# Quads of pool_out and down: another order of the seven products, their loads and sums, y pieces and squares at other steps, and a rewritten last normalization

## The reference, cut to what matters

```python
def pool_mixer(...):                       # ... mixed, scale, g are [256, 4096]
    return (mixed * scale * jax.nn.silu(g)) @ w_out          # y [256, 4096] @ w_out [4096, 2048]

def conv_ffn(...):                         # y [256, 5504] @ w_down [5504, 2048]
    ...

x = x + conv_ffn(rms_norm_2(x, norm_ffn[l]), w_up[l], conv_w[l], conv_b[l], w_down[l])
return rms_norm_2(x, norm_final)           # x * rsqrt(mean(x*x) + 1e-6) * g
```

## Time and profile before

| | |
|---|---|
| median of three runs | 2447.51 us (2446.94 to 2447.71) |
| profiled execution | 2447.4 us, its span 2445.6 us |
| TensorE busy | 2431.4 us, 12682 matmuls |
| VectorE busy | 1688.9 us |
| ScalarE busy | 1361.1 us |
| GpSimd busy | 64.3 us |
| granted TensorE clock | 0.999 |
| DMA | 453.03 MB, mean 185 GB/s |

### The profile page before, as it was taken

How to read it: one execution, slowest core, us unless ns; L and a number is a source line. 1 busy time by engine, 2 the same in 40 slices (tenths; PEclk the granted TensorE clock), 3 DMA queues, 4 the chain that set the end, 5 groups by cost and what they waited for, 6 DMA issues and landing times.

```text
span 2445.6 us, 34055 instructions
## 1 busy us (share of the span) xinstructions
PE 2431.4 (99%) x12682; PEld 2087.0 (85%) x12682; DVE 1688.9 (69%) x2037; ACT 1361.1 (56%) x1804; POOL 64.3 (3%) x79
## 2 busy tenths in 40 slices
PE   9999999999999999999999999999999999999998
PEld 8888888877889999888888888888988888888886
DVE  7675757899765655656656767665767667689886
ACT  6444444555656655556755556565644545456554
POOL 0000000001000000010000000000000000000010
PEclk9999999999999999999999999999999999999999
DMA  8666666565556654565585564455566666656654
GB/s 312 199 189 188 181 190 188 173 231 182 189 174 180 180 156 139 207 210 190 168 232 165 158 177 144 167 177 155 173 190 181 189 191 179 195 169 203 218 185 138
DMA packets 234627, 453.03 MB, mean 185 GB/s; under 512 B 14961, under 2 KB 60449, under 8 KB 233356
## 3 DMA queue, kind: packets, MB, share of 16 engines
q1 hardware_dynamic: 230992, 435.94, 57.3%
q0 software_dynamic: 3120, 14.90, 1.7%
q10 hardware_dynamic: 396, 0.59, 0.2%
HBM read 448.68 MB, written 2.69 MB: 185 GB/s over the span
## 4 chain that ended last, share of the span: by engine, by line
PE 95%; DVE 4%; ACT 1%; issue 0%; DMA 0%; SPq 0%; ACTq 0%; DVEq 0%
PE ps L779 24%; PE ps L781 13%; PE ps L745 12%; PE ps L747 12%; PE ps L746 12%; PE ps L929 4%; PE ps L931 4%; PE ps L930 4%; DVE w_lo L2361 1%; PE ps L703 1%; PE ps L812 1%; PE ps L811 1%; PE ps L810 1%; PE ps L1381 1%; DVE w_lo L2353 0%; PE ps L1141 0%
## 5 line engine op out<-in xcount | busy, mean ns | idle before, releaser
L2353 DVE TENSOR_TENSOR w_lo<-raw,w_hi 128x1024 fp32r<-128x1024 f32 x702 | 861.0, 1233 | 504.7 <-ACT w_hi L1551 484.0
L1551 ACT ACTIVATE w_hi<-raw 128x1024 fp32r<-128x1024 f32 x702 | 740.6, 1060 | 676.9 <-PE ps L781 357.2
L779 PE MATMUL ps<-x_hi_lo,w_hi 128*128 128x512 f32 x2336 | 820.9, 394 | 0.5 <-DVE w_lo L2353 0.5
L781 PE MATMUL ps<-x_hi_lo,w_lo 128*128 128x256 f32 x2336 | 660.7, 283 | 0.0
L779 PEld LDWEIGHTS ps<-x_hi_lo,w_hi 128*128 128x128 f32 x2336 | 438.7, 188 | 102.0 <-DVE w_lo L2353 0.8
L745 PE MATMUL ps<-w_hi,x_hi_lo 128*128 128x512 f32 (+3 forms) x1248 | 487.2, 390 | 0.0
L747 PE MATMUL ps<-w_hi,x_hi_lo 128*128 128x512 f32 (+3 forms) x1248 | 478.9, 384 | 0.0
L746 PE MATMUL ps<-w_lo,x_hi_lo 128*128 128x512 f32 (+3 forms) x1248 | 477.9, 383 | 0.0
L781 PEld LDWEIGHTS ps<-x_hi_lo,w_lo 128*128 128x128 f32 x2336 | 439.2, 188 | 0.0
L1728 ACT ACTIVATE w_hi<-raw 128x1024 fp32r<-128x1024 f32 (+1 forms) x184 | 189.2, 1041 | 164.4 <-PE ps L931 130.7
L747 PEld LDWEIGHTS ps<-w_hi,x_hi_lo 128*128 128x128 f32 x1248 | 234.5, 188 | 42.2
(11 more groups left out here) (442 smaller groups left out, 2563.3 us busy)
## 6 DMA issues: line engine op xcount, KB each, us to landing
raw<-in_w_up SPq DMA_DIRECT2D x160, 512.0 KB, 4.0
raw<-in_pool_w_in SPq DMA_DIRECT2D x126, 512.0 KB, 4.0
raw<-in_w_in SPq DMA_DIRECT2D x96, 480.0 KB, 3.7
raw<-in_w_down SPq DMA_DIRECT2D x82, 512.0 KB, 5.0
raw<-in_pool_w_out SPq DMA_DIRECT2D x64, 512.0 KB, 4.6
raw<-in_ple_w_gate SPq DMA_DIRECT2D x64, 512.0 KB, 4.2
raw<-in_mla_w_in SPq DMA_DIRECT2D x56, 448.0 KB, 3.5
raw<-in_pool_w_group SPq DMA_DIRECT2D x32, 512.0 KB, 4.1
```

The source lines that it names most:

```text
L779: pe.matmul(bank, w_hi[:, slot, cols], xs[:, k].rearrange("p s n -> p (s n)"), start=k == 0, stop=False, skip_group_check=True)
L781: last = pe.matmul(bank[:, 0:T], w_lo[:, slot, cols], xs[:, k, 0, :], start=False, stop=k == nkt - 1, skip_group_check=True)
L1551: act.activation(w_hi[:, t.slot(), :], raw[:, slot, :], ACT.Copy).then_inc(S("w_hi"), 1)
L2353: dve.tensor_tensor(w_lo[:, t.slot(), :], raw[:, u % RAW, :], w_hi[:, t.slot(), :].bitcast(F32), ALU.subtract)\
```

## The change

The quads' products go in the order b11, T2, b22, T3, T1, b21, T4 on all engines. The sums are formed as T2 = b22 - b12, T3 = T2 + b11, T1 = b22 - T3, T4 = b21 - T3. The four loads come as b12, b22, b11, b21, with another table of releases. The first quad of pool_out comes one plain step later in pair 0. TensorE waits for all banks of both sets at the first quad or the first plain step of the pair's second chunk, whichever comes first. The squares of columns 1 and 0 go behind later steps (pool_out: from 6, 7 to 15, 17; down: from 8, 9 to 23, 26), the y pieces of down behind steps 6, 7, 11, 13, 17, 22 instead of 6 to 11, and the first PSUM reads of pool_out's pair 0 one step later. In the ending the first three columns' sums and the 1e-6 are put together ahead for both halves, the root takes the last column's sum with scale 1/D and that as bias, and VectorE adds the second half's last columns between the two pieces it scales for the first half.

```diff
-POOL_OUT = [P0[:9] + PQ[0] + P1[:3] + PQ[1] + P1[3:6] + PQ[2] + P1[6:] + P0[9:],
+POOL_OUT = [P0[:9] + P1[:1] + PQ[0] + P1[1:4] + PQ[1] + P1[4:7] + PQ[2] + P1[7:] + P0[9:],
+DOWN_Y_STEPS = {6: 3, 7: 4, 11: 5, 13: 6, 17: 7, 22: 8}
@@ quad_tables
-                loads += [(j1, 2 * p), (j1, 2 * p + 1), (j2, 2 * p + 1), (j2, 2 * p)]
-                released += [products + 3, products + 3, products + 5, products + 6]
+                loads += [(j1, 2 * p + 1), (j2, 2 * p + 1), (j1, 2 * p), (j2, 2 * p)]
+                released += [products + 1, products + 4, products + 6, products + 6]
@@ tensor: quad
                     block(e1, "e1", x.yh[:, y1, t0], x.yl[:, y1, t0], last)
+                    block(e7, "e7", x.sums_hi[0][:, q], x.sums_lo[:, 0, q], last)
                     block(x.bank(c + 1, 0), (c + 1, 0), x.sums_hi[2][:, q], x.sums_lo[:, 2, q])
+                    block(e6, "e6", x.sums_hi[1][:, q], x.sums_lo[:, 1, q], last)
                     block(e5, "e5", x.yh[:, y1, t1], x.yl[:, y1, t1], last)
-                    block(e7, "e7", x.sums_hi[0][:, q], x.sums_lo[:, 0, q], last)
                     block(x.bank(c, 0), (c, 0), x.yh[:, y2, t0], x.yl[:, y2, t0])
-                    block(e6, "e6", x.sums_hi[1][:, q], x.sums_lo[:, 1, q], last)
                     block(x.bank(c, 1), (c, 1), x.yh[:, y2, t1], x.yl[:, y2, t1])
@@ tensor: the steps of a pair
                 for kind, c, kts in steps:
+                    if (kind == "quad" or c == 2 * p + 1) and begins("all sets"):
+                        for s in range(2):
+                            pe.wait_ge(S(f"mm_free{s}"), t.at(f"set{s}", 1))
...
-                        if c == 0:
-                            for s in range(2):
-                                pe.wait_ge(S(f"mm_free{s}"), t.at(f"set{s}", 1))
-                            if p == 0:
-                                pe.wait_ge(S(split), x.tiles.index("sums") + 1)
+                        if c == 0 and p == 0:
+                            pe.wait_ge(S(split), x.tiles.index("sums") + 1)
@@ scalar: step_hi
-                product_hi(loaded(0))
                 product_hi(loaded(2))
                 product_hi(summed(0, 1))
-                product_hi(summed(1, 2))
+                product_hi(loaded(1))
+                product_hi(summed(2, 2))
+                product_hi(summed(1, 3))
                 product_hi(loaded(3))
-                product_hi(summed(2, 3))
                 product_hi(summed(3, 4))
@@ scalar: squares and y pieces
-            if n == 6:
+            if n == 15:
                 square_mixed(1)
-            if n == 7:
+            if n == 17:
                 square_mixed(0)
...
-            if 6 <= n < 3 + len(DOWN_Y):
-                y_hi(n - 3)
+            if n in DOWN_Y_STEPS:
+                y_hi(DOWN_Y_STEPS[n])
...
-            if n in (8, 9):
-                square_out(9 - n)
+            if n in (23, 26):
+                square_out((26 - n) // 3)
@@ scalar: the ending
-            act.sem_inc(S("last_sums"), 1)
-            act.wait_ge(S("last_mean_square"), tt + 1)
-            act.activation(rt[:, 12, tt:tt + 1], ms[:, 12, tt:tt + 1], ACT.Sqrt).then_inc(S("last_root"), 1)
+            act.wait_ge(S("last_mean_square"), 1)
+            act.activation(rt[:, 12, tt:tt + 1], sums[:, 12, tt, 3:4], ACT.Sqrt, scale=1.0 / D, bias=ms[:, 12, tt:tt + 1])\
+               .then_inc(S("last_root"), 1)
@@ vector: step_lo
-            b11, b12, b22, b21 = (raw[:, (u + n) % RAW, :] for n in range(4))
-            product_lo(b11)
-            dve.wait_ge(S(f"raw_full{(u + 1) % RAW}"), 16 * ((u + 1) // RAW + 1))
-            dve.tensor_tensor(b11, b12, b11, ALU.subtract).then_inc(S("w_sums"), 1)
-            product_lo(b22)
+            b12, b22, b11, b21 = (raw[:, (u + n) % RAW, :] for n in range(4))
+            sums_before = t.n.get("w_sums", 0)
+            for n in range(2):
+                dve.wait_ge(S(f"raw_full{(u + n) % RAW}"), 16 * ((u + n) // RAW + 1))
             dve.tensor_tensor(b12, b22, b12, ALU.subtract).then_inc(S("w_sums"), 1)
             product_lo(b11)
+            dve.wait_ge(S("w_sums"), sums_before + 1)
+            dve.tensor_tensor(b11, b12, b11, ALU.add).then_inc(S("w_sums"), 1)
+            product_lo(b12)
+            product_lo(b22)
+            dve.wait_ge(S("w_sums"), sums_before + 2)
             dve.tensor_tensor(b22, b22, b11, ALU.subtract).then_inc(S("w_sums"), 1)
-            product_lo(b12)
+            product_lo(b11)
+            product_lo(b22)
             product_lo(b21)
-            dve.wait_ge(S("w_sums"), t.n.get("w_sums", 0) + 3)
-            dve.tensor_tensor(b21, b21, b22, ALU.subtract).then_inc(S("w_sums"), 1)
-            product_lo(b22)
+            dve.tensor_tensor(b21, b21, b11, ALU.subtract).then_inc(S("w_sums"), 1)
             product_lo(b21)
@@ vector: the ending
-        for tt in range(2):
+        link(dve.reduce_sum(ms[:, 12, :], sums[:, 12, :, 0:3], AXX))
+        dve.tensor_scalar(ms[:, 12, :], ms[:, 12, :], 1.0 / D, EPS, ALU.mult, ALU.add).then_inc(S("last_mean_square"), 1)
+        def last_columns(tt):
...
+        last_columns(0)
+        for tt in range(2):
             dve.wait_ge(S("last_root"), tt + 1)
             dve.reciprocal(rstd[:, 12, tt:tt + 1], rt[:, 12, tt:tt + 1]).then_inc(S("last_rstd"), 1)
             dve.wait_ge(S("last_rstd"), tt + 1)
+            dst = h[:, tt, 1024:1536]
+            dve.tensor_scalar(dst, dst, rstd[:, 12, tt:tt + 1], None, ALU.mult).then_inc(S("final_added_out"), 1)
+            if tt == 0:
+                last_columns(1)
+            dst = h[:, tt, cols]
+            dve.scalar_tensor_tensor(dst, dst, rstd[:, 12, tt:tt + 1], fgain[:, cols], ALU.mult, ALU.mult).then_inc(S("final_added_out"), 1)
```

More of the change, by code:

```diff
@@ L2830, in _ @@
                 y_lo(n - 4)
-            if n in (20, 21):
-                quads_mixed(0, n - 20)
+            if n in (21, 22):
+                quads_mixed(0, n - 21)
         for n in (2, 3):
@@ L3378, in _ @@
                 dve.wait_ge(S("y_pairs"), 15)
-            if 6 <= n < 3 + len(DOWN_Y):
-                y_lo(n - 3)
+            if n in DOWN_Y_STEPS:
+                y_lo(DOWN_Y_STEPS[n])
             if 28 <= n <= 28 + 3:
@@ L3402, in _ @@
             dve.tensor_tensor(h[:, tt, cols], h[:, tt, cols], down.bank(NCH - 1, tt), ALU.add).then_inc(S("last_added"), 1)
-            dve.wait_ge(S("last_sums"), tt + 1)
-            link(dve.reduce_sum(ms[:, 12, tt:tt + 1], sums[:, 12, tt:tt + 1, :], AXX))
-            dve.tensor_scalar(ms[:, 12, tt:tt + 1], ms[:, 12, tt:tt + 1], 1.0 / D, EPS, ALU.mult, ALU.add).then_inc(S("last_mean_square"), 1)
+        last_columns(0)
+        for tt in range(2):
             dve.wait_ge(S("last_root"), tt + 1)
```

## The result

The changed kernel takes 2453.40 us (median of 11 runs, 2452.87 to 2453.99), the kernel before 2447.51 (11 runs, 2446.85 to 2448.23): ratio 1.0024, 95% interval [1.0017, 1.0032]. I had forecast 2451.3, no change that can be told, in a range up to 2453.2; the measured time is just outside. The profiled execution of after took 2452.87 us, its span is 2451.1, 5.5 us longer than before's.

The account below looks back on a forecast made before the run. TensorE, busy 2431.4 of 2445.6 us, was taken to bound the kernel. Terms: +8.7 + 0.9 - 4.75 - 1.05 = +3.8 us on the profiled 2447.4, 2451.2, or 2451.3 from the median; range 2445.5 to 2453.2.

Parts of the forecast that it names:

- T4's chain: All 14 quads: T4's sum after product 5's w_lo delays product 6, 0.62 us a quad, +8.7 us (7.1 to 10.2).
- The stalls of before: TensorE's nine stalls in pool_out's and down's quads all go: -4.75 us (bounds -5.0 and -4.0).
- The y piece behind the first quad: pool_out's first pair: y_hi and y_lo come between products 6 and 7, +0.9 us with restart (bounds 0 and 1.2).
- The loads: New load order; tightest is the next quad's b11 in down, late by 0.4 to 0.9 us but absorbed: 0 us.
- The ending: After TensorE's last matmul: root starts 0.4 us earlier, second half's addition 0.65 earlier; -1.05 us (bounds -0.4 and -1.2).
- The squares moved: Squares of columns 1 and 0, moved after the last quad, cost nothing: ScalarE has 1.7 us of pause each plain step.
- The rival "more is late": Late b11 load in six quads of down, or quad 0's y piece, makes 1 us: 2454 and more; chance 0.08.
- the 1.1 us worked out there: By the skill's drain rule each sum starts 0.08 us later, total some 1.1 us higher; the prediction followed the trace.

Follow-up runs that it names:

- the exchange: The changed kernel with products 4 and 5 of each quad exchanged on all three engines: 2443.15 us, ratio to the kernel before 0.9982.
- the other slot: The changed kernel, product order kept, with T4 written into T2's raw slot (b12's) and its sum before product 5's w_lo: 2446.15 us, ratio 0.9996.
- the moves alone: The changed kernel with the old order of a quad's products, sums, loads and releases; moves and new ending stay: 2443.31 us, ratio 0.9983.
- Its repair by itself: The changed kernel with pool_out's y pieces 6 and 7 behind steps 11 and 12 instead of 10 and 11: 2453.03 us, ratio 1.0022.
- the order alone: The kernel before with only the new order of a quad's products, sums, loads and releases: 2459.89 us, ratio 1.0050.

## Why the prediction was wrong, point by point

- *T4's chain*: right in place, mechanism and size. 14 x 0.65 = 9.1 us against 8.7; a wait loses 0.54 us against 0.51, and the restart 0.11. The row of TensorE idles 0.38 us, 0.35 were forecast, and ScalarE waits 2.43 us for the fourth sum, 2.4 forecast. Shown by the exchange and, in down, by the other slot.
- *The stalls of before*: none is left at its former place, 4.7 us; shown by the moves alone.
- *The y piece behind the first quad*: 0.9 us, as forecast. Its repair by itself was not as I thought: 0.2 us by the trace.
- *The loads*: no cost in the change, as forecast: ScalarE waits once for a load of down, 2.0 us, and no wait of TensorE beyond the forecast ones stands in down. The slot freed late in one experiment shows where a cost may begin.
- *The ending*: -0.9 us against -1.05. The chain through VectorE and ScalarE gave what was forecast (the last scaling starts 1.09 us earlier); behind it 0.2 us came back, a term that I had at nothing in the sum. All eleven traces with the new ending have 6.0 to 6.1 us behind the last scaling's start, the two with the old one 5.8. Why is open.
- *The squares moved*: **this is the step that failed.** I wrote that in their new places "each plain step leaves ScalarE 2.79 - 1.06 = 1.7 us of pause, so they cost nothing". I looked for cover on ScalarE, although the sentence before it rests on the earlier trace rows, where GpSimd's multiplication, released by the squares, blocks VectorE; and I did not look at what VectorE does at step 14. I put at nothing what cost 1.44 + 0.10 = 1.5 us: in the new place GpSimd's multiplication meets VectorE's two rope instructions, 1.20 and 1.22 us instead of 0.23. Shown twice: with the squares later, and with only GpSimd's release later, the wait is gone (2451.76 and 2451.96 us).

The sum of the measured terms: 9.1 + 0.9 + 1.5 - 4.7 - 0.9 = +5.9 us, as between the medians, against +5.5 between the spans; the 0.4 lie in an earlier start of pool_out (0.2) and a pace of 0.2325 instead of 0.2328 us a matmul there (0.2), neither of which I can explain. Both are no larger than the differences between the other runs' traces: pool_out starts at 457.5 to 458.4 us in them, and its pace away from stalls is 0.2324 to 0.2328 us. Without the failed step and with 0.4 us less in T4's chain it is within 0.2 us of the forecast of +3.8. The rival "more is late" had the right direction, but it began at 2454, above the 2453.4 measured, and named the wrong places, the loads and the y piece.

The prediction sets a sentence of the Trainium skill ("VectorE: DVE Perf Modes", section "The DRAIN you can't avoid") against its row, and leaves out that the same paragraph goes on that a next operation which is not held starts earlier. So the early start of the sum does not contradict the page by itself, and the 1.1 us worked out there rest on half of its rule. The changed kernel shows the early start again: the w_lo at 528.27 is drawn to 529.50, the sum starts at 529.41.

## What to carry to other kernels

Where one engine bounds and others feed it through a few slots, write down for the last product of a group the whole chain from the freed slot, in the rows' durations; a value formed in place from a tile that is itself a late product puts two conversions in a row, and a neighbour that doesn't need it, written between them, takes the chain off the path. When work is moved, look at every engine that it releases: in their new places the squares cost ScalarE nothing that TensorE waited for, and 1.5 us through GpSimd on VectorE. And time a reordering by itself beside the moves that it comes with: here the moves were worth 4.2 us and hid that the order cost 10.

## What the runs showed of the hardware

Two VectorE instructions of 128 x 64 elements with two SBUF inputs took 1.20 and 1.22 us instead of 0.23 while GpSimd ran a multiplication of two SBUF tensors. The Trainium skill says on the page "SBUF — State Buffer", section "SBUF: two separate sides", that VectorE instructions with two SBUF inputs and GpSimd's share a port pair held for a whole instruction, and that the loser blocks fully. The trace agrees: each waited for the end of one of GpSimd's instructions (1.28 us each). A large one gained about as much, 1.22 to 2.31 us, so in these rows it was the small instruction that lost the larger share of its time.

One SBUF input is no protection by itself. A `tensor_scalar` of 128 x 2 elements took 1.17 us in the kernel before, where the median of that line is 0.17, beside another such multiplication:

```profile
635.18 1.17 DVE L2487 TENSOR_SCALAR mean_square<-mean_square 128x2 f32<-128x2 f32 x1
635.03 2.55 POOL L3445 TENSOR_TENSOR mixer_out<-mixer_out,post_gain 128x512 f32<-128x512 f32 x2 [8.99 <-ACTq L1842]
```

The `tensor_scalar` at 606.90 in the changed kernel took its usual 0.20 us, but it started before GpSimd's multiplication (606.93), and the one at 609.62 ran behind it; they say nothing of what would happen beside it. The reciprocal at 636.62 in the kernel before, one input too, took its usual 0.17 us with GpSimd at work. Which other instructions with one SBUF input are blocked these runs leave open.

A stall of TensorE cost 0.16 us more than its idle time in the trace: that is the overlap in which matmuls are drawn (0.39 us long at a pace of 0.2325). Then came 0.10 to 0.11 us between the next two matmuls, at every wait for w_lo with over 0.1 us of idle time in pool_out and down (7 of them before, 16 after, 19 with the order alone).
